# Modulation columns: sums in 32x32 squares on VectorE and a fold on TensorE, in place of four 128x128 tiles on TensorE

## The reference, cut to what matters

```python
c_act = jax.nn.silu(c)                      # [1, 1024]
mod = c_act @ w_ada + b_ada                 # w_ada [1024, 6144] for each layer
shift1, scale1, gate1, shift2, scale2, gate2 = jnp.split(mod, 6, axis=-1)
h = modulate(rms_norm(x, norm1_g), shift1, scale1)
```

```python
logits = logits + cum[:, :, q0:q1, None] - cum[:, :, None, :q1]
```

## Time and profile before

| | |
|---|---|
| three runs | 3006.54, 3006.74, 3011.04 us; median 3006.74 |
| the profiled execution | 3010.3 us, its span 3008.5 us |
| PE busy | 2951.7 us (98%), 15563 matmul passes |
| PEld busy | 2469.9 us (82%) |
| DVE / ACT / POOL busy | 1036.9 / 1089.7 / 1176.1 us |
| DMA | 315.34 MB, mean 105 GB/s |
| mean granted TensorE clock | 0.993 of full speed |

### The profile page before, as it was taken

The page is one execution under the profiler, slowest core; times in us unless marked ns, Lnnn a source line. Parts: engine busy times, 40 slices in busy tenths (PEclk is TensorE's granted clock), DMA queues, the critical chain, the costliest instruction groups (busy, mean ns, idle before and its releaser), DMA issues.

```text
span 3008.5 us, 36622 instructions
## 1 busy us (share of the span) xinstructions
PE 2951.7 (98%) x15563; PEld 2469.9 (82%) x15563; DVE 1036.9 (34%) x1822; ACT 1089.7 (36%) x1657; POOL 1176.1 (39%) x502
## 2 busy tenths in 40 slices
PE   7999999999999999999999999999999999999999
PEld 3877888898888888788898888988888877888887
DVE  2543354255554533242243220342110265521102
ACT  3424433243332433433234332333222266432221
POOL 1332235334445433234435444444444343344442
PEclk9999999999999999999999999999999999999999
DMA  6332245335555432123323333333333322233332
GB/s 216 98 98 64 71 154 154 86 116 186 188 182 182 109 77 68 50 84 98 98 78 111 94 95 97 95 92 98 96 95 95 93 78 69 70 96 96 98 96 73
DMA packets 523799, 315.34 MB, mean 105 GB/s; under 512 B 15954, under 2 KB 496884, under 8 KB 523380
## 3 DMA queue, kind: packets, MB, share of 16 engines
q1 hardware_dynamic: 523636, 313.00, 35.4%
HBM read 310.86 MB, written 2.10 MB: 104 GB/s over the span
## 4 chain that ended last, share of the span: by engine, by line
PE 94%; DVE 2%; DMA 2%; ACT 1%; issue 0%; SPq 0%; DVEq 0%; ACTq 0%
PE b L427 21%; PE b L429 21%; PE b L428 21%; PE o L427 5%; PE o L429 5%; PE o L428 5%; DMA raw<-in_w_in_dram 2%; PE b L468 1%; PE b L469 1%; PE b L470 1%; PE b L586 1%; PE o L769 1%; PE b L600 1%; PE s L652 1%; PE b L947 1%; PE b L948 0%
## 5 line engine op out<-in xcount | busy, mean ns | idle before, releaser
L2575 POOL TENSOR_TENSOR lo<-raw,hi 128x1024 fp32r<-128x1024 f32 (+1 forms) x492 | 1173.9, 2394 | 1794.1 <-ACT hi L1210 1793.7
L427 PE MATMUL b<-HH,hi 128*128 128x512 f32 x1792 | 713.7, 398 | 3.5 <-DVE rq L1987 3.0
L429 PE MATMUL b<-HH,lo 128*128 128x512 f32 x1792 | 699.1, 390 | 0.0
L428 PE MATMUL b<-HL,hi 128*128 128x512 f32 x1792 | 698.6, 390 | 0.0
L1210 ACT ACTIVATE hi<-raw 128x1024 fp32r<-128x1024 f32 (+1 forms) x492 | 508.9, 1039 | 460.2 <-DMA raw<-in_w_down_dram 106.1
L427 PEld LDWEIGHTS b<-HH,hi 128*128 128x128 f32 x1792 | 336.9, 188 | 82.5 <-issue 12.5
L429 PEld LDWEIGHTS b<-HH,lo 128*128 128x128 f32 x1792 | 336.8, 188 | 71.9
L428 PEld LDWEIGHTS b<-HL,hi 128*128 128x128 f32 x1792 | 337.0, 188 | 71.0 <-issue 2.2
L427 PE MATMUL b<-FH,hi 128*128 128x512 f32 (+1 forms) x594 | 218.0, 367 | 0.0
L429 PE MATMUL b<-FH,lo 128*128 128x512 f32 (+1 forms) x594 | 217.1, 365 | 0.0
L428 PE MATMUL b<-FL,hi 128*128 128x512 f32 (+1 forms) x594 | 217.0, 365 | 0.0
(11 more groups left out here) (460 smaller groups left out, 4504.6 us busy)
## 6 DMA issues: line engine op xcount, KB each, us to landing
raw<-in_w_ada_dram SPq DMA_DIRECT2D x96, 512.0 KB, 4.9
raw<-in_w_up_dram SPq DMA_DIRECT2D x88, 512.0 KB, 3.9
raw<-in_w_in_dram SPq DMA_DIRECT2D x80, 512.0 KB, 4.4
raw<-in_w_mg_dram SPq DMA_DIRECT2D x48, 512.0 KB, 3.8
raw<-in_ffn_w_gate_dram SPq DMA_DIRECT2D x44, 512.0 KB, 3.8
raw<-in_ffn_w_up_dram SPq DMA_DIRECT2D x44, 512.0 KB, 3.8
raw<-in_w_down_dram SPq DMA_DIRECT2D x32, 512.0 KB, 4.0
raw<-in_ffn_w_down_dram SPq DMA_DIRECT2D x32, 512.0 KB, 3.9
```

The costliest lines, as they stand in the source:

```text
L427: e.matmul(out, wh, xh, start=start and k == 0, stop=False)
L428: e.matmul(out, wh, xl, start=False, stop=False)
L429: mm = e.matmul(out, wl, xh, start=False, stop=stop and k == last)
L2575: e.tensor_tensor(t["lo"][:, s, 0:w], K.raw[:, s, 0:w], t["hi"][:, s, 0:w].bitcast(F32), ALU.subtract).then_inc(*m.lo.up(n))
```

## The change

For the 20 rows of `ada`, VectorE does two more operations once `AA` is complete. The first transposes `AA` in squares of 32x32: within a quarter of the partitions (32 of them), partition and column change places inside each square. It writes into the last chunk's slot of `raw`, which is why that chunk is released by the second operation and no longer by L1955. The second adds up each run of 32 columns, so `AS` [128 x 16] holds, on partition 32 a + i and in column b, the sum over the 32 partitions of quarter a of `AA`'s column 32 b + i. TensorE then adds the four quarters a and puts the results in place: `fold` is four 32x32 identities one below the other, and for each output quarter c a matmul with `fold` as weight (32 columns) takes the four columns c, c+4, c+8, c+12 of `AS`. `ada_row` and `ada_columns` stay for the first four rows of layer 0.

The table `sel` (512 columns) leaves the constants and `fold` (32) comes in, so `CON` has 774 columns in place of 1254. `bias` takes its weight from a column of `ident`, repeated 128 times by a stride of zero.

```diff
-       ("CT", 64), ("sel", 512), ("pick", 36)]
+       ("CT", 64), ("fold", 32), ("pick", 36)]
...
-    out["sel"] = np.concatenate([np.zeros((96, 512)), np.repeat(np.eye(4), 128, axis=1), np.zeros((28, 512))])
+    out["fold"] = np.tile(np.eye(32), (4, 1))
...
# TensorE, ada
-        self.ada_columns(l, q_, self.m.vnorm.at("ada", l, q_, 7), 128)
+        self.ada_fold(l, q_)
+
+    def ada_fold(self, l, q_):
+        e, q, m, t = self.e, self.q, self.m, self.t
+        b = self.take_bank(("col", l, q_))
+        q.wait_ge(m.vnorm.at("ada", l, q_, "s"), self.free[b])
+        for c in range(4):
+            mm = e.matmul(self.bank[b][32 * c:32 * c + 32, 0:4], t["fold"], t["AS"][:, c:16:4], start=True, stop=True)
+        mm.then_inc(*m.stat.up(("col", l, q_)))
+        self.free[b] = m.vnorm.at("mod", l, q_)
...
# TensorE, bias
-            e.matmul(bank["o"][:, :], t["sel"][:, h * 128:h * 128 + 128], t["FFT"][:, :], start=True,
+            e.matmul(bank["o"][:, :], bc(t["ident"][:, 96 + h:97 + h], 128), t["FFT"][:, :], start=True,
...
# VectorE, ada
-                done = [("ada", l, q_, kk)] + ([("chunk", n)] if k else [])
+                done = [("ada", l, q_, kk)] + ([("chunk", n)] if k and g < 3 else [])
...
+            if g == 3:
+                self.ada_sums(l, q_, n, raw[:, 0:512])
...
+    def ada_sums(self, l, q_, n, room):
+        e, q, m, t = self.e, self.q, self.m, self.t
+        q.wait_ge(m.vnorm.at("ada", l, q_, 7))
+        e.transpose(room, t["AA"][:, :]).then_inc(*m.vnorm.up(("ada", l, q_, "t")))
+        q.wait_ge(m.vnorm.at("ada", l, q_, "t"))
+        e.tensor_reduce(t["AS"][:, :], room.rearrange("p (b i) -> p b i", i=32), AXX, ALU.add).then_inc(
+            *m.vnorm.up(("ada", l, q_, "s"), ("chunk", n)))
...
+        fixed("AS", [128, 16])
```

## The result

The changed kernel took 2992.61 us, median of 4 runs (2989.33 to 2995.28), where the kernel before took 3008.3 beside it (4 runs, 3006.54 to 3011.04). The ratio is 0.9949, with a 95% interval of 0.9936 to 0.9962: faster by half a per cent, with the sign forecast. The gain is 15.7 us where the forecast has 9.4, and the time lies 1.2 us under the lower end of the range. The forecast is thus wrong in size. A second and a third measurement of the same kernel gave ratios of 0.9973 and 0.9964.

The account below looks back on a forecast made before the run. TensorE's work was taken to bound the kernel. Fold 9.0 us plus constants 0.6 less waits 0.2 gave 9.4 us off the median of 3006.74: 2997.3 us, range 2993.8 to 3003.5.

Parts of the forecast that it names:

- the fold's saving: TensorE's modulation sums in 20 rows: 0.45 us less a row, 9.0 us in all, bounds 4.4 to 10.0.
- What bounds the kernel: TensorE, busy 2951.7 of 3008.5 us: work taken from it counts in full, VectorE's only where TensorE waits.
- The passes: Eight fold passes a row: 0.10 us first to last, tail 0.13, dense weights loaded in the open 0.20.
- the list of signs: Expected in the profile: among others, passes about 0.25 us a row in the chain, the dense one behind 0.43.
- Rival 1: Fold passes do not run beside each other, 0.68 us a row or slightly more: 3001.9 us, chance 0.12.
- Rival 2: TensorE reaches other engines' results or loads sooner, giving back 3 to 5 us: 3001 to 3002, chance 0.08.
- rival 3: TensorE waits for VectorE's two additions: slower, 3023 us if GpSimd always keeps both out; chance 0.05.
- VectorE's two operations: Between the end of the sums and TensorE's use: 0.70 us each, 1.5 us a row, bounds 1.2 and 5.6.
- The waits: TensorE waiting for VectorE in layer 1's last row and gated rows: 0.2 us, bounds 0 to 3.
- The loads: SyncE's queue: last chunk released 1.5 us later, six waits maybe 1.5 us longer each; no term.
- The constants: Load at the kernel's start, 246 KB less: TensorE starts earlier, 0.6 us gained, bounds 0.3 to 0.9.
- The bias: Matmuls taking their weight from ident by a stride of zero: same passes and columns, no effect.

Follow-up runs that it names:

- e5: Kernel before with only the narrow constants and bias from ident, plus 64 idle bytes so the tile region begins at 127104: 3002.93 us, ratio 0.9993.
- e8: Changed kernel without VectorE's two operations, AS set to zero, so the sums over columns are missing: 2995.87 us, ratio 0.9961.
- e3: Changed kernel unedited, measured a second time: 2997.53 us, ratio 0.9973.
- e12: Changed kernel unedited, measured a third time: 2996.53 us, ratio 0.9964.
- e9: Changed kernel with VectorE's two operations kept, but TensorE summing AA the old way after waiting for them: 3005.38 us, ratio 0.9997.
- e10: Changed kernel with all four products of the fold written to one quarter, the other three left out: 2999.76 us, ratio 0.9978.
- e2: Changed kernel with 448 idle columns in the constants, so the load is nearly as wide as before: 2996.33 us, ratio 0.997.
- e4: Changed kernel with each row's fold and bias addition moved one program step later, into the next row: 2996.97 us, ratio 0.9967.
- e1: Kernel before with only the narrow constants and bias from ident, the tile region then beginning at 126976: 3021.65 us, ratio 1.0054.
- e6: Changed kernel with only the region of working tiles moved by 128 bytes: 3013.18 us, ratio 1.0021.
- e7: Changed kernel with every tile of the partition moved by 128 bytes: 2992.13 us, ratio 0.9954.
- e11: Changed kernel with the fold one step later and every tile moved by 128 bytes: 2991.82 us, ratio 0.9953.

## Why the prediction was wrong in size, and what it had right

**The step that failed** is the size of the fold's saving. The prediction took 0.45 us a row, 9.0 us in all, with 10.0 as the most; the runs show 0.55 us a row, 11.0 us (11.4 by e5 and e8, 10.8 and 11.2 by the profiles of e5 against e3 and e12). These are 2.0 of the 4.7 us between the 2997.3 of the forecast and the 2992.6 of the first measurement. The other terms nearly cancel. The rest is chance in the four runs, and the range had too little for it: their median lies 3.0 us under the changed kernel's own mean at equal clock (about 1.9 us of it by their mean clock of 0.9948 against 0.994, the rest beyond it), where the forecast had allowed 2. With 11.0 as the bound of the fold the lower end would have been 2992.8, still 0.2 us above what came out.

**What bounds the kernel: right.** TensorE's list of work is the time. A fold that is 0.55 us shorter shows as 0.55 us in every row that does not wait, and the 28 us of VectorE's new operations cost next to nothing (e9: 0.9).

**The passes: the mechanism right, the term too small.** I took 0.45 us a row with a bound of 0.50; it is 0.52 by the chain and 0.55 by the starts of the later passes. Of the three parts, the load of the dense weights in the open is right (0.20: the dense pass counts 0.43). The first to the last pass was put at 0.10 and is 0.07, the tail at 0.13 and is 0.11, and "passes count about 0.25 us a row" in the list of signs is 0.18. The parts as they were added up gave 0.47, and 0.45 was taken after a scaling of L505. The bound was at fault too: it held L1142's tail fixed and gave the quarters only 0.03 to gain, and what came is past it. 20 x 0.1 = 2.0 us of the miss. The edge behind the fold is that which "TensorEngine Tiling (Array Packing)" of the Trainium skill, section Key Properties, gives for a change of tiling mode (TensorE drains); the trace agrees, 0.43 against 0.34 behind L600, though no run tells a drain from another cause of it. Section Instruction Overhead of the same page has about 60 cycles of overhead for each matmul, and warns against tiling a dimension that is small; of passes in quarters of their own the trace shows 10 ns from one to the next, so the warning does not bind here.

**Rival 1, passes one behind the other: out.** It had 43 ns from one to the next; e10 is the kernel in which they share a quarter, and even there they are 34 ns apart. Rival 2 (3 to 5 us back as waits) and rival 3 (TensorE waits for both additions) are out too: 2.4 us is the most that any profile shows, and no row of the feed-forward part waits.

**VectorE's two operations: right.** 1.5 us a row forecast, 1.47 in all rows, and the transpose at 0.71 as the price taken from the reduction. The upper bound, both kept out by GpSimd, never occurred.

**The waits: 0.2 us taken, 2.4 in the first profile, 1.0 in e2's, none in the other five.** The place was named (the two gated rows and a chance collision), and the 0 to 3 us of the bound hold it. In the two rows of the first profile the older sums, not the new operations, meet GpSimd, and their 2.0 us come on top of the chain. At the last row the distance was used up to 0.1 us, as forecast. The average over the seven profiles is 0.5 us; e4 and e8 lie 1.5 and 2.2 us under the changed kernel, each with an uncertainty of about 1, so the price is not known better than that.

**The loads: right, no term.** SyncE's waits for VectorE at the chunks grew from 11.8 us to the 23.9 of these two lines, somewhat more than the 6 x 1.5 us that were named, and laid pass by pass beside before TensorE is nowhere later for it:

```profile
SPq L2620 <- DVE AA L1965: 14.2, 4, 7.1
SPq L2620 <- DVE AS L1980: 9.7, 4, 3.5
```

**The constants: 0.6 taken,** 1.08 in the first pair, 0.6 as the mean of the loads of all profiles (4.16 against 4.74 us). What the start then keeps of it can't be told: the sums of the fourth row begin at 55.5 us in before and at 54.7 in e2, and at 53.0 to 55.5 in the narrow kernels. The half that I took off for a later rise of the clock is neither shown nor refuted, since that rise itself moves by more from execution to execution. e5 (1.6 at equal clock, with an uncertainty near 1) agrees with either. **The bias: nothing, right** (e5).

**What was not in the sum: the clock's chance.** The range had 2 us for the scatter of a median. Two executions of one program differ in how many stretches of 3.4 us they run at half clock behind pauses of TensorE, each for 1.7 us, and in the profiled pair this was 5.1 us for the change. It is no effect of the change: the mean clock of before's 58 runs is 0.9941, that of the changed kernel's 19 runs 0.9937. With the terms as the traces have them the forecast would have been 3006.7 - (11.0 + 0.6 - 0.5) = 2995.6, and the mean of all 19 runs is 2996.3 (2995.6 at equal clock). That the point of 2997.3 lies within 2 us of this is in part luck: the fold was taken 2.0 us too small. "TensorE: Matmul & The Clock Gate" of the Trainium skill, Part 1, says of the slow stretch at a kernel's start that it differs from run to run and costs less than 1% of a typical span. The traces agree (16 passes in 8.28 to 9.63 us for e12 and e3, where full clock has 6.96, under 0.1% of the span). The later stretches of before come to 12 us, 0.4% (23.9 us at half clock), and here that is as much as the whole change.

**What the prediction never looked at: where the tiles begin.** The change moves the region of working tiles by 1792 bytes, which is seven times 256. That it kept its place against the other tiles is luck: in e1 it begins 128 bytes lower, and there the dense passes lose 19 us, more than the fold gains.

## What to carry to other kernels

Sums over the columns of a 128x512 tile are cheap for a VectorE with room, 1.4 us in two operations, and the 128x128 weight loads that they spare TensorE count in full wherever TensorE is always busy. Before a gain of a few microseconds is read off two medians, put the runs to one granted clock, and repeat the measurement; and take no term of a microsecond from a single pair of profiles before the same rows have been compared between two executions of one kernel. And when an edit changes the size of a tile, look at where all tiles behind it now begin: here 64 idle bytes were worth more than the edit under study.

## What the runs showed of the hardware that was not expected

- Dense passes of 128x512 that read tiles in a region beginning 128 bytes off the others (modulo 256) follow each other at 229 to 238 ns, not 227: about 19 us in all (e1 against e5, e6 against the changed kernel), and none of it when the 128 bytes are made equal again (e5, e7). "SBUF — State Buffer" of the Trainium skill, section Operand start alignment, asks for a multiple of the element's size and says that its tests timed nothing; e1 and e6 keep that rule and are slow.
- Two kernels with all tiles at multiples of 256 bytes were 3 to 4 us under their like at equal clock (e7, e11). The cause is open.
- The first 16 passes of the program took from 8.28 us (e12) to 9.63 us (e3) in two executions of one kernel, and the constants' load 4.04 and 4.43 us; the mean granted clock holds neither.
- Four-column passes with 32-column weights start 10 ns apart on average when they write quarters of their own, 34 ns when they share one (e10).
- VectorE's transpose of 128x512 in squares of 32 takes 0.71 us, also where it lies wholly within an operation of GpSimd (two rows of the first profile, four of e3), while a sum with two sources, 0.75 us by itself, took up to 2.96 us beside such an operation.
